# Expert-choice layers: the prompt's routed rows handled in groups of up to eight experts instead of expert by expert

## The reference, cut to what matters

```python
def expert_choice_ffn(h, router, e_gate, e_up, e_down):
    b, t, _ = h.shape
    cap = EC_FACTOR * t // N_EXPERTS
    aff = jax.nn.softmax(jnp.einsum('btd,de->bte', h, router).astype(jnp.float32), axis=-1)
    gate, idx = lax.top_k(jnp.swapaxes(aff, 1, 2), cap)
    xe = h[bidx, idx]
    hid = jax.nn.silu(jnp.einsum('becd,edf->becf', xe, e_gate)) * jnp.einsum('becd,edf->becf', xe, e_up)
    ye = jnp.einsum('becf,efd->becd', hid, e_down) * gate[..., None].astype(h.dtype)
    return jnp.zeros_like(h).at[bidx, idx].add(ye)
# x = x + gt2 * expert_choice_ffn(h, ...), for the sample rows and, with their own gt2, for the prompt rows
```

## Time and profile before

| | us |
|---|---|
| median of 3 runs | 3958.61 (3956.07 to 3959.44) |
| the profiled execution | 3956.13, its span 3954.4 |
| TensorE busy | 3578.8 (91% of the span) |
| TensorE weight loads | 3118.8 (79%) |
| VectorE, ScalarE, GpSimd busy | 1311.3, 650.1, 189.7 (33%, 16%, 5%) |
| moved by DMA | 664.33 MB, mean 168 GB/s |
| granted TensorE clock, mean | 0.953 of full |

### The profile page before, as it was taken

One profiled execution on the slowest core, in us unless ns is written; L12 is line 12 of the kernel. 1 busy time (PEld: TensorE's weight loads), 2 busy tenths in 40 slices (PEclk: granted clock), 3 DMA queues, 4 the chain that ended last, 5 costly groups with the idle time before them and its releaser, 6 DMA issues. The chain is left out here.

```text
span 3954.4 us, 81654 instructions
## 1 busy us (share of the span) xinstructions
PE 3578.8 (91%) x36990; PEld 3118.8 (79%) x36990; DVE 1311.3 (33%) x3130; ACT 650.1 (16%) x1649; POOL 189.7 (5%) x150
## 2 busy tenths in 40 slices
PE   5979798897979988739999999999999999999995
PEld 2467494775935554439999999999999999999995
DVE  3476777767634443451111111111111111111112
ACT  2222323222214452200000000000000000000001
POOL 0000101001010000000000000000000000000000
PEclk7989899998989989869999999999999999999997
DMA  7200000000031103149878787877878787878772
GB/s 315 59 8 12 12 4 20 3 16 12 4 89 30 30 2 112 70 149 347 267 262 268 261 273 264 268 264 267 270 267 267 266 271 261 269 262 268 262 262 107
DMA packets 498248, 664.33 MB, mean 168 GB/s; under 512 B 31134, under 2 KB 436950, under 8 KB 494830
## 3 DMA queue, kind: packets, MB, share of 16 engines
q1 hardware_dynamic: 492094, 640.18, 48.3%
q0 software_dynamic: 5632, 18.88, 1.8%
q10 hardware_dynamic: 176, 0.05, 0.0%
HBM read 630.70 MB, written 28.36 MB: 167 GB/s over the span
## 5 line engine op out<-in xcount | busy, mean ns | idle before, releaser
L1990 PE MATMUL bank<-e_hid,e_wd 128*128 128x144 f32 x5632 | 760.1, 288 | 0.0
L1978 PE MATMUL bank<-e_xT,e_wg 128*128 128x144 f32 x5632 | 749.5, 286 | 1.0 <-ACT e_xT L2032 1.0
L1978 PE MATMUL bank<-e_xT,e_wu 128*128 128x144 f32 x5632 | 748.2, 286 | 0.0
L2075 DVE TENSOR_TENSOR e_tm<-bank,e_sg 128x144 f32<-128x144 f32 x352 | 108.4, 308 | 1852.9 <-ACT e_sg L2039 1852.9
L1978 PEld LDWEIGHTS bank<-e_xT,e_wg 128*128 128x128 f32 x5632 | 715.5, 190 | 1.0 <-issue 1.0
L1990 PEld LDWEIGHTS bank<-e_hid,e_wd 128*128 128x128 f32 x5632 | 710.5, 190 | 5.6
L1978 PEld LDWEIGHTS bank<-e_xT,e_wu 128*128 128x128 f32 x5632 | 714.5, 190 | 0.0
L2039 ACT ACTIVATE e_sg<-bank 128x144 f32<-128x144 f32 x352 | 102.5, 291 | 1998.2 <-PE bank L1978 1998.2
L519 PE MATMUL bank<-hT_x,wblk 128*128 128x512 f32 (+1 forms) x672 | 237.2, 512 | 10.0 <-DMA wblk<-in_w_in 8.6
L519 PEld LDWEIGHTS bank<-hT_x,wblk 128*128 128x128 f32 x672 | 115.6, 199 | 125.0 <-issue 113.3
L661 PE MATMUL bank<-r_TW,r_X 64*64 64x64 f32 x2880 | 167.6, 220 | 4.3 <-DVE r_X L1073 1.3
(11 more groups left out here) (314 smaller groups left out, 3518.5 us busy)
## 6 DMA issues: line engine op xcount, KB each, us to landing
e_wg<-in_e_gate SPq DMA_DIRECT2D x176, 1024.0 KB
e_wu<-in_e_up SPq DMA_DIRECT2D x176, 1024.0 KB
e_wd<-in_e_down SPq DMA_DIRECT2D x176, 1024.0 KB
h_wmod<-in_w_mod SPq DMA_DIRECT2D x24, 1024.0 KB, 18.3
wblk<-in_w_in SPq DMA_DIRECT2D x22, 512.0 KB
h_x<-in_x_sample SPq DMA_DIRECT2D x8, 512.0 KB, 7.5
wo<-in_w_out SPq DMA_DIRECT2D x2, 2048.0 KB, 11.3
o_x<-in_x_sample SPq DMA_DIRECT2D x8, 512.0 KB
```

What stands on the lines that cost most here:

```text
L1978: last = nc.tensor.matmul(bank[6 + b % 2][:, j * TOK:(j + 1) * TOK], w[s][:, k, f], xT[e % 2][:, k, :], start=(k == 0), stop=(k == KD - 1))
L1990: last = nc.tensor.matmul(bank[k // PER_BANK][:, c:c + TOK], wd[s][:, b % DUO, k * P:(k + 1) * P], hid[:, b % 2, :], start=(b == 0 and k % ...
L2075: V.tensor_tensor(tm[b % 2][:, :], bank[6 + b % 2][:, 0:TOK], sg[b % 2][:, :], ALU.mult)\
```

## The change

In topk the prompt's two rounds now come first. When they are done, SP stores the prompt's lists (16 experts x 16) to memory while VectorE goes on with the sample, and reads them back as K.idxq and K.gateq: one column for each half of the experts, expert and place within its 16 on 128 partitions.

In experts one indirect DMA gathers the prompt rows of eight experts (128 rows) into xp. prompt_token turns them with eight 128x128 transposes into xpT; VectorE copies 16 columns of it into each expert's xT. This is done ahead of expert 0 and, for experts 8 to 15, during expert 7. On the way back VectorE collects each expert's 16 columns of yT in ypT; prompt_output turns them for experts 0 to 7 during expert 8, and for 8 to 14 during expert 15. prompt_scaled scales them all at once. Expert 15 has its own eight transposes (output_last_prompt) behind the last block. The adding DMAs into ffnp stay one for each expert, each behind the landing of the one before (scp): eight in a row for the first group, issued in GpSimd's step for expert 9, seven in a row for the second, issued while expert 15 is computed, and one at the end. The sample's sums have a chain of their own (sc). gt2p is spread over 128 partitions instead of 16. xe's transposes now fill the banks 3 and 4 alone, so ScalarE copies bank 3 and VectorE bank 4; output no longer waits between its halves.

The diff, cut to its core:

```diff
+        prompt_ok, listed, loaded = K.sem("k_prompt_ok"), K.sem("k_listed"), K.sem("k_loaded")
         with nc.Block() as block:
+            @block.sync
+            def _(sp):
+                sp.wait_ge(prompt_ok, 1)
+                sp.dma_start(K.dram["idxq"][:, :], idx[:, CAP:TOK]).then_inc(listed, 16)
+                sp.dma_start(K.dram["gateq"][:, :], val[:, CAP:TOK]).then_inc(listed, 16)
+                sp.wait_ge(listed, 32)
+                for dst, name in ((K.idxq, "idxq"), (K.gateq, "gateq")):
+                    sp.dma_start(dst[:, :], bass.AP(tensor=K.dram[name].tensor, offset=0, ap=[[1, P], [P, 2]]),
+                                 allow_slow_non_contiguous=True).then_inc(loaded, 16)
+                sp.wait_ge(loaded, 32)
+
             @block.vector
             def _(dve):
                 V = nc.vector
                 link = Link(dve, chain)
-                for at, n, col, cap in ((0, NS, 0, CAP), (NS, NP, CAP, CAPP)):
+                for at, n, col, cap in ((NS, NP, CAP, CAPP), (0, NS, 0, CAP)):
+                    if at == 0:
+                        dve.sem_inc(prompt_ok, 1)
...
-        xe, xp = sb("xe", [P, D]), sb("xp", [CAPP, D])
+        xe, xp = sb("xe", [P, D]), sb("xp", [P, D])
+        xpT = sb("xpT", [P, KD, P])
         xT = [sb(f"xT{i}", [P, KD, TOK]) for i in range(2)]
         sg = [sb(f"sg{i}", [P, TOK]) for i in range(2)]
         tm = [sb(f"tm{i}", [P, TOK]) for i in range(2)]
         hid = sb("hid", [P, 2, TOK])
         yT = sb("yT", [P, KD, TOK])
-        ye, yp = sb("ye", [P, D]), sb("yp", [CAPP, D])
+        ypT = sb("ypT", [P, KD, P])
+        ye, yp = sb("ye", [P, D]), sb("yp", [P, D])
         gt2 = sb("gt2", [P, D])
-        gt2p = sb("gt2p", [CAPP, D])
+        gt2p = sb("gt2p", [P, D])
...
+        GROUP = ((0, 8), (8, 15))
+        HALF = KD // 2
+
+        def part(e):
+            return slice((e % 8) * CAPP, (e % 8 + 1) * CAPP)
...
-                            sp.dma_start(gt2p[:, :], mod_row(K, GT2, 1, CAPP)).then_inc(rows, 16)
+                            sp.dma_start(gt2p[:, :], mod_row(K, GT2, 1)).then_inc(rows, 16)
 
             @block.gpsimd
             def _(pool):
                 def gather(e):
-                    for dst, src, ix in ((xe, K.dram["h2d"], K.idx), (xp, K.dram["h2p"], K.idxp)):
-                        pool.indirect_dma_start(out=dst[:, :], out_offset=None, in_=src[:, :],
-                                                in_offset=bass.IndirectOffsetOnAxis(ap=ix[:, e:e + 1], axis=0))\
-                            .then_inc(x_in, 16)
+                    pool.indirect_dma_start(out=xe[:, :], out_offset=None, in_=K.dram["h2d"][:, :],
+                                            in_offset=bass.IndirectOffsetOnAxis(ap=K.idx[:, e:e + 1], axis=0))\
+                        .then_inc(x_in, 16)
+
+                def gather_prompt(g):
+                    pool.indirect_dma_start(out=xp[:, :], out_offset=None, in_=K.dram["h2p"][:, :],
+                                            in_offset=bass.IndirectOffsetOnAxis(ap=K.idxq[:, g:g + 1], axis=0))\
+                        .then_inc(xp_in, 16)
+
+                def scatter_prompt(e):
+                    if e:
+                        K.hold(pool, scp, 16 * e)
+                    rows = part(e) if e < NE - 1 else slice(0, CAPP)
+                    pool.indirect_dma_start(out=K.dram["ffnp"][:, :],
+                                            out_offset=bass.IndirectOffsetOnAxis(ap=K.idxp[:, e:e + 1], axis=0),
+                                            in_=yp[rows, :], in_offset=None, compute_op=ALU.add).then_inc(scp, 16)
 
                 gather(0)
+                gather_prompt(0)
                 K.hold(pool, x_ps, 1)
                 gather(1)
+                K.hold(pool, xp_ps, 2)
+                gather_prompt(1)
                 for e in range(NE):
                     if e + 2 < NE:
                         K.hold(pool, x_ps, e + 2)
                         gather(e + 2)
-                    K.hold(pool, s_ok, 4 * e + 4)
+                    for g, (first, last) in enumerate(GROUP):
+                        if e == last + 1 or (e == last and last == NE - 1):
+                            K.hold(pool, sp_ok, 2 * g + 2)
+                            for i in range(first, last):
+                                scatter_prompt(i)
+                    K.hold(pool, s_ok, 2 * e + 2)
                     if e:
-                        K.hold(pool, sc, 32 * e)
-                    for src, dst, ix in ((ye, K.dram["ffn"], K.idx), (yp, K.dram["ffnp"], K.idxp)):
-                        pool.indirect_dma_start(out=dst[:, :],
-                                                out_offset=bass.IndirectOffsetOnAxis(ap=ix[:, e:e + 1], axis=0),
-                                                in_=src[:, :], in_offset=None, compute_op=ALU.add).then_inc(sc, 16)
-                K.hold(pool, sc, 32 * NE)
+                        K.hold(pool, sc, 16 * e)
+                    pool.indirect_dma_start(out=K.dram["ffn"][:, :],
+                                            out_offset=bass.IndirectOffsetOnAxis(ap=K.idx[:, e:e + 1], axis=0),
+                                            in_=ye[:, :], in_offset=None, compute_op=ALU.add).then_inc(sc, 16)
+                K.hold(pool, sp_ok, 6)
+                scatter_prompt(NE - 1)
+                K.hold(pool, scp, 16 * NE)
+                K.hold(pool, sc, 16 * NE)
...
-                        pe.wait_ge(x_in, 32 * e + 32)
+                        pe.wait_ge(x_in, 16 * e + 16)
                         if e >= 2:
-                            pe.wait_ge(s_ok, 4 * e - 4)
-                    b, c = 3 + k // PER_BANK, (k % PER_BANK) * TOK
-                    nc.tensor.transpose(bank[b][:, c:c + CAP], xe[:, k * P:(k + 1) * P], K.ident[:, :])
-                    last = nc.tensor.transpose(bank[b][:, c + CAP:c + TOK], xp[:, k * P:(k + 1) * P],
-                                               K.ident[0:CAPP, 0:CAPP])
+                            pe.wait_ge(s_ok, 2 * e - 2)
+                    last = nc.tensor.transpose(bank[3 + k // HALF][:, (k % HALF) * P:(k % HALF + 1) * P],
+                                               xe[:, k * P:(k + 1) * P], K.ident[:, :])
                     if k == KD - 1:
                         last.then_inc(x_ps, 1)
+
+                def prompt_token(g, k, b):
+
+                    if k == 0:
+                        pe.wait_ge(xp_in, 16 * g + 16)
+                    if k == HALF and g:
+                        pe.wait_ge(xp_ok, 2 * g + 1)
+                    last = nc.tensor.transpose(bank[b][:, (k % HALF) * P:(k % HALF + 1) * P], xp[:, k * P:(k + 1) * P],
+                                               K.ident[:, :])
+                    if k % HALF == HALF - 1:
+                        last.then_inc(xp_ps, 1)
+
+                def prompt_output(g, k):
+
+                    if k == 0:
+                        pe.wait_ge(yc_ok, GROUP[g][1])
+                        pe.wait_ge(xp_ok, 2 * len(GROUP))
+                    if k == HALF:
+                        pe.wait_ge(sp_ok, 2 * g + 1)
+                    n = (GROUP[g][1] - GROUP[g][0]) * CAPP
+                    last = nc.tensor.transpose(bank[5][0:n, (k % HALF) * P:(k % HALF + 1) * P], ypT[:, k, 0:n],
+                                               K.ident[:, :])
+                    if k % HALF == HALF - 1:
+                        last.then_inc(yp_ps, 1)
...
-                    if k == 4:
-                        pe.wait_ge(s_ok, 4 * e + 2)
-                    c = slice((k % 4) * P, (k % 4 + 1) * P)
-                    nc.tensor.transpose(bank[3 + k // 4][:, c], yT[:, k, 0:CAP], K.ident[:, :])
-                    last = nc.tensor.transpose(bank[5][0:CAPP, c], yT[:, k, CAP:TOK], K.ident[:, :])
-                    if k % 4 == 3:
+                    last = nc.tensor.transpose(bank[3 + k // HALF][:, (k % HALF) * P:(k % HALF + 1) * P], yT[:, k, 0:CAP],
+                                               K.ident[:, :])
+                    if k % HALF == HALF - 1:
                         last.then_inc(y_ps, 1)
+
+                def output_last_prompt(k):
+
+                    last = nc.tensor.transpose(bank[5 + k // HALF][0:CAPP, (k % HALF) * P:(k % HALF + 1) * P],
+                                               yT[:, k, CAP:TOK], K.ident[:, :])
+                    if k % HALF == HALF - 1:
+                        last.then_inc(yp_ps, 1)
 
                 for k in range(KD):
                     token(0, k)
+                for k in range(KD):
+                    prompt_token(0, k, 5 - 3 * (k // HALF))
...
+                        if e == GROUP[0][1] - 1 and b in (2, 3, 4, 5, 9, 10, 11, 12):
+                            prompt_token(1, b - 2 if b < 6 else b - 5, 5)
+                        for g, (first, last) in enumerate(GROUP):
+                            if e == last and b in (4, 5, 6, 7, 10, 11, 12, 13):
```

(56 more changed lines are left out.)

9 lines of the change are left out of this document (7 added, 2 removed).

## The result

The changed kernel takes **3891.73 us** (median of 4 runs, 3889.64 to 3893.43), the kernel before 3957.34 in the same series (3954.26 to 3959.44): a ratio of 0.9835, 95% interval 0.9818 to 0.9852. The profiled execution took 3890.84 us with a span of 3889.1, against 3956.13 and 3954.4.

A forecast was written before the change was run, and what follows sets the result against it. TensorE was taken as the bound; blocks -53.8, tail -2.9 and head -0.5 us sum to -57.2, which from the median of before, 3958.61, gives 3901.4 us (-1.4%), range 3893 to 3915.

The forecast's parts named there:

- Bound and price of the pieces: Expert blocks: two transposes cost 0.47 us in a token block, 0.22 in an output block; removing narrow ones gives -53.8 us.
- New waits of TensorE: Inside the expert blocks: each new wait looks satisfied beforehand, taken at nothing; otherwise under 1 us, four times.
- VectorE's additions: Expert blocks: added copies and scalings, at most about 1.1 us in one block, stay hidden.
- rival 5: Experts 7, 8 and 15: a wide gather or copy comes late for TensorE, +24 us, 3926; chance 0.02.
- Chains of the prompt's sums: GpSimd's chained DMAs, eight from expert 9 and seven in expert 15, stay hidden, the second with 4.6 us margin.
- rivals 1 and 4: Seven-DMA chain outlasts expert 15: 3910 to 3924 us, chance 0.09; or makes the kernel slower than before, 3966, chance 0.01.
- Tail: After the last down matmuls: earlier scaling and sums, -2.9 us, with bounds -3.5 and 0.
- Head: From the experts' start to the first gate_up: -0.5 us, with bounds -2 and +3.
- The failed step: The sum had no term for the stages ahead of topk, and topk itself was put at 0.
- 3 us from run to run: Part of the forecast range's downward side: 3 us allowed for differences between runs.
- The base: The median of before, 3958.61 us, from which the forecast difference of -57.2 us was counted.

The follow-up runs named there:

- no_narrow_token: The kernel before, leaving out the narrow transposes of xp for experts 1 to 15: 3912.11 us, ratio 0.9895.
- narrow_with_128_partitions: The kernel before, with the narrow transpose of xp written as a plain product of a zero-filled 128-partition operand: 3938.45 us, ratio 0.9962.
- front_with_tiles: The kernel before without topk and experts, with the change's two small tiles reserved and unused: mean 1693.6 us, against 1698.3 without the tiles.

## Why the prediction was right in part and wrong in its sum

- **Bound and price of the pieces: right.** TensorE is the bound: busy in every microsecond from 2000 us on, to 3900 before and to 3800 after, at a granted clock of 1.00, so what left its sequence came off the end. -52.75 us in the blocks, of which the slower clock takes back 0.3 (the second group of matmuls lasts 3.16 at a mean granted clock of 0.67 instead of 2.85 at 0.74), so -53.05 against -53.8. The rest is within the rounding of the spacings, 0.01 us on 240 pieces. Reading the 0.47 of a token block as 0.11 and 0.36 was an argument in the prediction; no_narrow_token and narrow_with_128_partitions show it, as far as the 16 partitions go.
- **New waits of TensorE, VectorE's additions: right.** Between the first gate_up and the last down matmul no wait is left in the timeline of PE, and rival 5 falls with it. The prediction's 1.1 us inserted in one block isn't three times 0.73, as it says; the largest pair of copies measured is 0.68 + 0.38 = 1.06 us (a half of xT and the prompt's columns).
- **Chains of the prompt's sums: right that they hide, wrong in size.** The period was put at 5.4 us, from a landing of 4.5 measured behind a larger DMA. Alone it is 3.9, and the margin 16 us instead of 4.6, so rivals 1 and 4 fall. The last one, again behind the sample's sum, landed in 4.7.
- **Tail: right.** -3.0 against -2.9, step for step: scaling starts 0.69 behind the first transpose, the sample's sum is issued 0.89 behind it, the prompt's 1.87 later. The pair is at the low end: from the first of the last transposes to the last prompt sum's issue it is 7.86 to 8.74 us in the six traces without the change and 4.86 or 4.87 in the four with it.
- **Head: right in sign, too small.** -2.1, with the 0.3 given back later -1.8, against -0.5. The term that was mis-sized is the landing of the wide gather. It was put at 8.1 or 10.1 us after its issue and taken in the middle, 9.1; it was issued at 1731.95, and its transposes ran at 1739.88 straight behind the others without a wait, so it had landed within 7.9.
- **The failed step: what lies ahead of topk was put at nothing.** The sum starts at the stage of topk and takes all ahead of it as unchanged, since no instruction of it changes. The runs showed two things in its place. The diff reserves two tiles ahead of all stages, and these moved the big tiles to better addresses, which is worth 4 to 5 us on average (2.7 in the output stage of the profiled pair). And the last 60 us of attention differ by 3.7 to 4.6 us with the clock of the execution; in the profiled pair after had 3.8 less. The "3 us from run to run" in the range is less than this clock alone brings, and front_with_tiles spreads over 6 us between executions (1690.64 to 1696.97).
- **The base failed as much.** The forecast was set on a median of three, 3958.61; the mean of 32 later runs is 3954.29. From that base the forecast difference gives 3897.1, and the measured mean of after is 3891.16: 5.9 short, 1.7 behind the turn and 4.2 ahead of it. So the 9.7 us by which 3891.73 lies below 3901.4 are 4.3 of base, 4.2 ahead of the turn, 1.7 behind it, less 0.6, as that median is above the mean. On the base of 32 runs the same range would be 3888.7 to 3910.7, and the measured time would lie in it: that it lies outside is in part the chance of three runs.
- **Open.** The last stretch is 0.9 us shorter, mostly between the issue of the last prompt sum and the first load of the last stage. That is an effect of the change and no chance: 10.96 to 11.29 us in the six traces without it, 10.12 to 10.21 in the four with it. Its cause is not shown.
